# A hybrid decoder layer on one core: every tensor in SBUF at another address

## The chip, the cores and the metric

The kernel runs on one core of a Trainium2 chip. The metric is the device time of the whole program in microseconds (us), from one launch to its end; lower is better. Beside the timed runs there is one profiled execution, from which all rows come.

## The reference

One layer of a decoder trunk on a sequence of 1024 positions with 1024 channels, in float32. Cut to what matters:

```python
hn   = rms_norm(x, norm_mix)
proj = hn @ w_in + b_in            # 1024 x 9728: x_rnn, z_rnn, q/k/v of 12 heads, z_att, two gates
xc   = causal_depthwise_conv(x_rnn)                    # 4 taps, 1280 channels
y_rnn = rg_lru(xc, ...) * silu(z_rnn)                  # block-diagonal gates, a scan over time
att  = merge of dilated_window_attention, 3 groups x 4 heads, dilations 1, 4, 16
y_att = att * silu(z_att)
merged = gates[0] * (y_rnn @ w_o_rnn) + gates[1] * (y_att @ w_o_att)
x = x + merged @ w_out
x = x + sigmoid(rms_norm(x) @ w_ple_gate + b) * (p @ w_ple)
```

## The kernel before, in words

Every large product is made from three passes. Each float32 operand is cut into a high part in TensorE's float32r format and the rest of it (`..._hi`, `..._lo`), and `passes` (lines 1144, 1148 and 1149) multiplies high by high, high by low and low by high. One pass is a weight load of 128 x 128 values and a matmul with 512 moving columns.

Weights come from HBM in 221 pieces of 128 x 512. SyncE loads them into `raw` (4 buffers, line 428 and 451), GpSimd cuts them (line 469 makes the high part, line 465 the low part) into `ring`, which has 16 slots (12 in the attention stage). TensorE gives a slot back when its last pass has started.

The stages follow one another in TensorE's program: 16 matmuls on zeros in `warm` (line 1208); transposes of the normed input, whose parts go to `hn_hi` and `hn_lo`; ten recurrent blocks j (projections with `hn` moving and weights stationary, then the gate products of `xc_hi` and `xc_lo`; VectorE and ScalarE do the convolution, the gates and the scan, and ScalarE spills `y_hi` and `y_lo` to HBM); 72 slots of q, k and v, where `hn` is stationary and the weights move. There dilation group 0 takes 128 adjacent positions of `hn` as a stationary block, group 1 takes every fourth position and group 2 every eighth. The attention steps (transposes at line 1256 and 1276, scores at 1267, values at 1287) are laid between these blocks in an order written out by hand. Then come 40 slots of gates and z, whose gates go to HBM through `g_out`; the output products in three stages of 16 (stationary weights, moving `ya`, `yra`, then `yrb` and `yrc`), for which ScalarE's queue loads the gates into `g_in` and the spilled y into `yra`, `yrb`, `yrc`; `w_out`; and the last products with `m_hi`, `m_lo`, `pT_hi`, `pT_lo`, whose results leave through `fin`.

All waits are semaphores set by hand. Nothing in the program reads an address, or waits because of one.

SBUF is laid out by hand too. `at(name, shape, dt, off)` places a tensor at `base + off`, the same in all 128 partitions, and tensors of stages that are over are overlaid. The offsets hang on a few marks: `H` (hn and what follows it there), `RW` (`raw`), `R` (`ring`), `E` (the attention stage's tensors, from ring slot 12 on), `X` (all else), `C` (small constants). In this build the first free byte (`nc.sbuf_base`) is 16481, so `base` is 16896, a multiple of 512.

Of the kernel before, what the change touches and what calls it, by code (L numbers as in the profile page):

```python
# [7 lines left out]
F32 = mybir.dt.float32  # L8
F32R = mybir.dt.float32r
# [3 lines left out]
P = 128  # L13
S = 1024
D = 1024
HALF = 512
# [3 lines left out]
NJ = RNN // P  # L20
# [26 lines left out]
RAW = 4  # L47
# [131 lines left out]
def build_layer(nc, a):  # L179
    stack = ExitStack()  # L180
    with stack:
# [1 line left out]
            return stack.enter_context(nc.semaphore(name))  # L183


        base = (nc.sbuf_base + 511) // 512 * 512

        def at(name, shape, dt, off):
            return nc.alloc_sbuf_tensor_at(name, shape, dt, offset=base + off)

        H, RW = 0, 65536
        R = RW + RAW * HALF * 4
        E = R + RING_Q * 2 * HALF * 4
        X = R + RING * 2 * HALF * 4
        C = X + 71680

        ident = at("ident", [P, P], F32, C)
        bias_in = at("bias_in", [P, 76], F32, C + 512)
        chan = at("chan", [P, 8, NJ], F32, C + 832)
        gain_mix = at("gain_mix", [P, KD], F32, C + 1152)  # L200
        eps_t = at("eps_t", [P, 1], F32, C + 1184)
        ssq_x = at("ssq_x", [P, NT], F32, C + 1216)
        std_x = at("std_x", [P, NT], F32, C + 1248)
# [1 line left out]
        half_x = at("half_x", [P, NT], F32, C + 1440)  # L205
        c_pos = at("c_pos", [P, NJ], F32, C + 1312)
        c_neg = at("c_neg", [P, NJ], F32, C + 1376)
        sp_t = at("sp_t", [P, 6, NJ], F32, X + 66560)

        hn_hi = at("hn_hi", [P, KD, S], F32R, H)  # L210
        hn_lo = at("hn_lo", [P, KD, S], F32R, H + 32768)
        ring = at("ring", [P, RING, 2, HALF], F32R, R)
        raw = at("raw", [P, RAW, HALF], F32, RW)
# [11 lines left out]
        a2buf = at("a2buf", [P, S], F32, X + 28704)  # L225
        ibuf = at("ibuf", [P, 2, S], F32, X + 32800)
        sgbuf = at("sgbuf", [P, 2, S], F32, X + 40992)
        y_hi = at("y_hi", [P, S], F32R, X + 49664)
        y_lo = at("y_lo", [P, S], F32R, X + 53760)
        xc_hi = at("xc_hi", [P, S], F32R, X + 57856)  # L230
        xc_lo = at("xc_lo", [P, S], F32R, X + 61952)

        qkv = at("qkv", [P, 3, NT, CHUNK, HD], F32, E)
        qkT = at("qkT", [P, 2, S], F32, E + 49152)
# [1281 lines left out]
```

## Time and profile before

| | |
|---|---|
| median of 3 runs | 1381.62 us (1379.93 to 1383.23) |
| the profiled execution's own time | 1379.93 us |
| its span, first to last instruction | 1378.1 us |
| TensorE busy | 1357.6 us (99%) |
| VectorE busy | 846.1 us (61%) |
| GpSimd busy | 490.5 us (36%) |
| ScalarE busy | 455.5 us (33%) |
| DMA, mean over the span | 101 GB/s |
| TensorE's granted clock, mean | 0.999 |

The profile calls TensorE's matmuls PE and its weight loads PEld, VectorE DVE, ScalarE ACT, GpSimd POOL. Matmuls are pipelined, so the duration of one is longer than the distance from its start to the next one's; it is that distance that counts for the time.

### The profile page before, as it was taken

To read this page: it belongs to the slowest core of one execution; us is meant where nothing else is said; L and a number is where in the kernel's file an instruction comes from. 1 tells how busy PE (TensorE), PEld (TensorE's weight loads), DVE (VectorE), ACT (ScalarE), POOL (GpSimd) and SP (SyncE) were. 2 spreads that over 40 slices of the span, in tenths; PEclk is the share of its full clock that TensorE was granted. 3 is DMA by queue.
4 is the path that set the end of the run, shared out by engine and by line. 5 is a ranking of instruction groups with operands and counts; after the bars stand their busy time and mean duration, and the time that the engine had idled before them with its cause. 6 is when DMAs were issued, how large, how long until landed. Compare 5 with 4: busy or idle time off the path is not lost.

```text
span 1378.1 us, 17897 instructions
## 1 busy us (share of the span) xinstructions
PE 1357.6 (99%) x6254; PEld 1168.1 (85%) x6254; DVE 846.1 (61%) x1674; ACT 455.5 (33%) x1157; POOL 490.5 (36%) x448
## 2 busy tenths in 40 slices
PE   8899999999999999999999999999999999999998
PEld 6688888888788999999999888888888788888887
DVE  6999998843768677685867774048612457235323
ACT  7354646532433343333423377211100001223100
POOL 6765424504404133040413432334057326044020
PEclk9999999999999999999999999999999999999999
DMA  6322222322202021120212132365459744221111
GB/s 241 93 84 77 95 74 77 107 94 70 77 8 85 19 90 55 38 78 16 84 39 60 63 108 87 109 207 200 139 191 412 250 132 131 92 77 52 48 46 46
DMA packets 76137, 139.51 MB, mean 101 GB/s; under 512 B 9649, under 2 KB 28817, under 8 KB 76049
## 3 DMA queue, kind: packets, MB, share of 16 engines
q10 hardware_dynamic: 31840, 75.56, 15.1%
q1 hardware_dynamic: 44208, 62.82, 15.0%
q8 instruction: 50, 0.82, 0.3%
q14 instruction: 39, 0.31, 0.1%
HBM read 108.84 MB, written 29.51 MB: 100 GB/s over the span
## 4 chain that ended last, share of the span: by engine, by line
PE 89%; DVE 7%; DMA 1%; issue 1%; ACT 1%; POOL 0%; POOLq 0%; DVEq 0%; ACTq 0%
PE bank L1144 28%; PE bank L1149 27%; PE bank L1148 27%; PE bank L1287 2%; PE bank L1267 2%; PE bank L1256 1%; DVE qkr L972 1%; DMA g_in<-gate_dram 1%; DVE qkn L957 1%; DVE qks L969 1%; PE bank L1276 1%; DVE qks L970 1%; DVE xc L872 1%; PE bank L1378 1%; DVE qkr L968 0%
## 5 line engine op out<-in xcount | busy, mean ns | idle before, releaser
L465 POOL TENSOR_TENSOR ring<-raw,ring 128x512 fp32r<-128x512 f32 x221 | 315.2, 1426 | 824.4 <-PE bank L1149 766.1
L1144 PE MATMUL bank<-hn_hi,ring 128*128 128x512 f32 x640 | 251.7, 393 | 1.2 <-DVE hn_lo L816 1.2
L1149 PE MATMUL bank<-hn_hi,ring 128*128 128x512 f32 x640 | 249.4, 390 | 0.0
L1148 PE MATMUL bank<-hn_lo,ring 128*128 128x512 f32 x640 | 249.1, 389 | 0.0
L1144 PE MATMUL bank<-ring,hn_hi 128*128 128x512 f32 x576 | 244.1, 424 | 0.2 <-POOL ring L465 0.2
L1148 PE MATMUL bank<-ring,hn_hi 128*128 128x512 f32 x576 | 229.6, 399 | 0.0
L1149 PE MATMUL bank<-ring,hn_lo 128*128 128x512 f32 x576 | 229.5, 398 | 0.0
L469 POOL TENSOR_SCALAR ring<-raw 128x512 fp32r<-128x512 f32 x221 | 181.6, 822 | 7.7 <-DMA raw<-in_w_rnn_s 7.7
L1148 PEld LDWEIGHTS bank<-ring,hn_hi 128*128 128x128 f32 x576 | 160.3, 278 | 7.1
L1149 PEld LDWEIGHTS bank<-ring,hn_lo 128*128 128x128 f32 x576 | 159.1, 276 | 7.7
L1144 PEld LDWEIGHTS bank<-ring,hn_hi 128*128 128x128 f32 x576 | 158.5, 275 | 7.6 <-POOL ring L465 0.6
L1144 PEld LDWEIGHTS bank<-hn_hi,ring 128*128 128x128 f32 x640 | 120.4, 188 | 25.5 <-POOL ring L465 1.4
L1149 PEld LDWEIGHTS bank<-hn_hi,ring 128*128 128x128 f32 x640 | 120.1, 188 | 25.4
L1148 PEld LDWEIGHTS bank<-hn_lo,ring 128*128 128x128 f32 x640 | 120.3, 188 | 24.4
L849 DVE TENSOR_TENSOR qkv<-bank,bias_qkv 128x512 f32<-128x512 f32 x72 | 49.6, 690 | 138.7 <-PE bank L1149 138.6
L579 ACT ACTIVATE sq_junk<-qkv 128x128 f32<-128x128 f32 x192 | 57.5, 300 | 158.0 <-DVE qkv L849 145.3
L1144 PE MATMUL bank<-ring,m_hi 128*128 128x512 f32 x256 | 100.4, 392 | 0.0
L1149 PE MATMUL bank<-ring,m_lo 128*128 128x512 f32 x256 | 99.7, 389 | 0.0
L1148 PE MATMUL bank<-ring,m_hi 128*128 128x512 f32 x256 | 99.6, 389 | 0.0
L617 ACT ACTIVATE probs<-scores,neg_max 128x128 f32<-128x128 f32 (+1 forms) x96 | 43.4, 452 | 134.4 <-DVE neg_max L983 134.2
L957 DVE SCALAR_TENSOR_TENSOR qkn<-qkv,rstd_qk,gain_qk 128x128 f32<-128x128 f32 x192 | 83.3, 475 | 0.4
L980 DVE CUSTOM_DVE_ANT_0 scores<-bank,masks 128x128 f32<-128x128 f32 (+1 forms) x96 | 33.3, 347 | 47.8 <-PE bank L1267 47.8
(176 smaller groups left out, 2129.2 us busy)
## 6 DMA issues: line engine op xcount, KB each, us to landing
raw<-in_w_tail_s SPq DMA_DIRECT2D x104, 256.0 KB, 2.7
g_in<-gate_dram ACTq DMA_DIRECT2D x48, 256.0 KB, 3.0
raw<-in_w_rnn_s SPq DMA_DIRECT2D x45, 256.0 KB, 2.6
raw<-in_w_qkv_s SPq DMA_DIRECT2D x48, 192.0 KB, 2.4
gate_dram<-g_out ACTq DMA_DIRECT2D x32, 256.0 KB, 2.1
raw<-in_w_qkv_s SPq DMA_DIRECT2D x48, 128.0 KB, 2.2
o_dram<-o_buf ACTq DMA_DIRECT2D x24, 256.0 KB, 2.0
o_in<-o_dram ACTq DMA_DIRECT2D x12, 512.0 KB, 4.1
```

The costliest lines, as they stand in the source:

```text
L465: nc.gpsimd.tensor_tensor(ring[:, ring_slot(p), 1], raw[:, p % RAW], ring[:, ring_slot(p), 0].bitcast(F32), ALU.subtract).then_inc(w_ready, 1)
L469: nc.gpsimd.tensor_scalar(ring[:, ring_slot(p), 0], raw[:, p % RAW], 1.0, 1.0, ALU.mult, ALU.mult).then_inc(hi_cut, 1)
L579: ins = nc.scalar.activation(sq_junk[:, i], qkv[:, c % 3, s, b], ACT.Square, accum_out=ssq_qk[:, u % HEADS, s, x:x + 1])
L617: nc.scalar.activation(probs[:, g % 2, c0:], scores[:, g % 2, c0:], ACT.Exp, bias=neg_max[:, g:g + 1], accum_out=den[:, g:g + 1]).then_inc ...
L849: V.tensor_tensor(qkv[:, c % 3, s].rearrange("p b d -> p (b d)"), bank[(N_A + T) % 4][:], bias_qkv[:, c % 2], ALU.add).then_inc(qkv_done, 1)
L957: ins = V.scalar_tensor_tensor(qkn[:, w].rearrange("p a b -> p (a b)"), qkv[:, c % 3, s, b], rstd_qk[:, s, w:w + 1], gain_qk[:, grp, w], A ...
L980: link(V.tensor_tensor_reduce(out=scores[:, g % 2, c0:], in0=bank[5][:, c0:2 * P], in1=masks[:, c0:2 * P] if grp < 2 else masks[:, 2 * P:] ...
L1144: ins = T.matmul(out, lhs[0], rhs[0], start=first, stop=False)
L1148: T.matmul(out, lhs[0], rhs[1], start=False, stop=False)
L1149: return T.matmul(out, lhs[1], rhs[0], start=False, stop=last)
L1267: T.matmul(bank[5][:, 0 if prev else P:2 * P], qkT[:, 0, tile * P:(tile + 1) * P], qkT[:, 1, k0:(tile + 1) * P], start=True, stop=True).th ...
L1287: ins = T.matmul(bank[7][:, 0:P], qkv[:, c % 3, tile - 1 + b, vb], probsT[:, g % 2, b * P:(b + 1) * P], start=b == parts[0], stop=b == 1)
```

## The change

The change moves tensors in SBUF. It rounds the base to 32 bytes instead of 512, puts the small constants (1728 bytes from mark C on, with `sp_t` now among them) between `raw` and `ring` instead of behind everything, and places `y_hi`, `y_lo`, `xc_hi` and `xc_lo` 32 bytes further up within their region.

```diff
-        base = (nc.sbuf_base + 511) // 512 * 512
+        base = (nc.sbuf_base + 31) // 32 * 32
...
-        R = RW + RAW * HALF * 4
+        C = RW + RAW * HALF * 4
+        R = C + 1728
         E = R + RING_Q * 2 * HALF * 4
         X = R + RING * 2 * HALF * 4
-        C = X + 71680
...
-        sp_t = at("sp_t", [P, 6, NJ], F32, X + 66560)
+        sp_t = at("sp_t", [P, 6, NJ], F32, C + 1472)
...
-        y_hi = at("y_hi", [P, S], F32R, X + 49664)
-        y_lo = at("y_lo", [P, S], F32R, X + 53760)
-        xc_hi = at("xc_hi", [P, S], F32R, X + 57856)
-        xc_lo = at("xc_lo", [P, S], F32R, X + 61952)
+        y_hi = at("y_hi", [P, S], F32R, X + 49696)
+        y_lo = at("y_lo", [P, S], F32R, X + 53792)
+        xc_hi = at("xc_hi", [P, S], F32R, X + 57888)
+        xc_lo = at("xc_lo", [P, S], F32R, X + 61984)
```

With 16481 as the first free byte, `base` becomes 16512. What each tensor's start leaves over when it is divided by 512, worked out from these offsets:

| tensors | before | after |
|---|---|---|
| `hn_hi`, `hn_lo`, `raw`, `yra`, `yrb`, `m_hi`, `pT_hi`, `pT_lo`, `ident` | 0 | 128 |
| `ring`, `x_nat`, `qkv`, `qkT`, `qkn`, `qkr`, `o_buf`, `ya_hi`, `yrc`, `m_lo`, `msum`, `g_in`, `fin` | 0 | 320 |
| `xc_hi`, `xc_lo`, `y_hi`, `y_lo` | 0 | 352 |
| `xc`, `rbuf`, `tbuf`, `abuf`, `a2buf`, `ibuf`, `sgbuf`, `warm` | 32 | 352 |
| `g_out`, `bias_qkv` | 192 | 0 |

## Rows read from the trace of the kernel before

**Rows 1.** The page: span; busy time, share, instructions; chain that ended last, by engine.

```profile
span 1378.1 us, 17897 instructions
...
PE 1357.6 (99%) x6254; PEld 1168.1 (85%) x6254; DVE 846.1 (61%) x1674; ACT 455.5 (33%) x1157; POOL 490.5 (36%) x448
...
PE 89%; DVE 7%; DMA 1%; issue 1%; ACT 1%; POOL 0%; POOLq 0%; DVEq 0%; ACTq 0%
```

**Rows 2.** Line 1144 over the whole span: length, PE busy (count), clock, DMA share, GB/s.

```profile
0.00:1378.10 1378.10, 712.11 (x1768) 1.00 0.30 101
```

**Rows 3.** Timeline of PE in attention group 0, first and last of 29 passes: start, duration.

```profile
299.46 0.39 PE L1144 MATMUL bank<-ring,hn_hi 128*128 128x512 f32 x1
...
305.81 0.39 PE L1148 MATMUL bank<-ring,hn_hi 128*128 128x512 f32 x1
```

**Rows 4.** Timeline of PE in groups 1 (6 passes) and 2 (12 passes).

```profile
454.94 0.39 PE L1144 MATMUL bank<-ring,hn_hi 128*128 128x512 f32 x1
...
456.11 0.40 PE L1149 MATMUL bank<-ring,hn_lo 128*128 128x512 f32 x1
...
639.69 0.41 PE L1144 MATMUL bank<-ring,hn_hi 128*128 128x512 f32 x1
...
642.40 0.41 PE L1149 MATMUL bank<-ring,hn_lo 128*128 128x512 f32 x1
```

**Rows 5.** The warm-up matmuls: all 16, then single ones by start.

```profile
1.31 6.03 PE L1208 MATMUL bank<-warm 128*128 128x512 bf16 x16 [1.31 <-POOL warm L459]
...
1.71 0.63 PE L1208 MATMUL bank<-warm 128*128 128x512 bf16 x1
...
5.98 0.50 PE L1208 MATMUL bank<-warm 128*128 128x512 bf16 x1
...
6.31 0.38 PE L1208 MATMUL bank<-warm 128*128 128x512 bf16 x1
...
6.96 0.38 PE L1208 MATMUL bank<-warm 128*128 128x512 bf16 x1
```

**Rows 6.** Groups by line and shape, VectorE and ScalarE: busy us, mean ns | idle before.

```profile
L849 DVE TENSOR_TENSOR qkv<-bank,bias_qkv 128x512 f32<-128x512 f32 x72 | 49.6, 690 | 138.7 <-PE bank L1149 138.6
...
L1113 DVE TENSOR_TENSOR fin<-bank,bias_ple 128x512 f32<-128x512 f32 x16 | 11.1, 691 | 68.0 <-PE bank L1149 68.0
...
L546 ACT ACTIVATE rbuf<-bank,chan 128x512 f32<-128x512 f32 x20 | 13.8, 690 | 3.3 <-DVE ibuf L905 3.3
...
L507 ACT ACTIVATE hn_hi<-bank,gain_mix 128x512 fp32r<-128x512 f32 x16 | 9.8, 689 | 5.0 <-PE bank L1185 4.9
```

**Rows 7.** Waits: engine line <- what it waited for: us in total, times, longest.

```profile
POOL ring L465 <- PE bank L1149: 766.1, 71, 48.1
...
PE bank L1144 <- POOL ring L465: 0.2, 1, 0.2
```

**Rows 8.** 1024 to 1080 us: length, PE, PEld, DVE, ACT, POOL busy, clock, DMA share, GB/s.

```profile
1024.00:1080.00 56.00, 56.00 (x248) 46.37 (x248) 13.09 (x19) 0.00 (x0) 38.07 (x41) 1.00 1.04 408
```

**Rows 9.** Timeline where that stretch ends: a gate load in the chain, VectorE and TensorE.

```profile
1064.43 16.61 DMA g_in<-gate_dram
...
1081.06 0.69 DVE L1062 TENSOR_TENSOR g_in<-bank,g_in 128x512 f32<-128x512 f32 x1 [12.24 <-DMA g_in<-gate_dram]
...
1080.50 0.39 PE L1149 MATMUL bank<-yra,ring 128*128 128x512 f32 x1
1081.81 0.50 PE L1144 MATMUL bank<-yra,ring 128*128 128x512 f32 x1 [0.92 <-DVE g_in L1062]
```

**Rows 10.** DMA, 3.0 us around one store of `o_buf`: its queue, share of 16 engines; landing.

```profile
q10 hardware_dynamic: 144, 0.26, 22.6%
...
o_dram<-o_buf ACTq DMA_DIRECT2D x1, 256.0 KB, 2.0
```

**Rows 11.** The same around one store of `g_out`, from 881.4 us.

```profile
q10 hardware_dynamic: 144, 0.26, 23.3%
...
gate_dram<-g_out ACTq DMA_DIRECT2D x1, 256.0 KB, 2.0
```

**Rows 12.** Timeline of the end: the last two stores are issued.

```profile
1374.39 1.67 ACTq L791 DMA_DIRECT2D out<-fin  x2
1374.99 0.69 DVE L1125 TENSOR_TENSOR fin<-fin,x 128x512 f32<-128x512 f32 x1
```

## The prediction

> **What bounds the kernel now.** First the page's busy times, then the chain that ended last: TensorE is busy for 99% of the span and makes up 89% of the chain; VectorE is 7% of it [rows 1]. So the time is the number of TensorE's instructions by the distance between them, plus a few waits. Line 1144, one of the three passes, runs 1768 times [rows 2]; lines 1148 and 1149 run as often, so there are 5304 passes. Their distance is read from starts in the timeline. In attention group 0 it is (305.81 - 299.46) / 28 = 0.2268 us [rows 3]; 5304 x 0.2268 = 1203 us, 87% of the span. 512 columns at 2.4 GHz, the level that the granted clock of 1.00 [rows 2] stands for, are 0.2133 us, so 0.0135 us per pass is something else. Because every pass counts, the question for a change of addresses is whether a pass, a packet or a vector instruction depends on where its operand begins. What a third of a nanosecond per pass is worth (5304 x 0.0003 = 1.6 us) shows how sharp that question is.
>
> **The change part by part.** Instructions, semaphores, queues and DRAM addresses stay the same; only starts in SBUF move. Nothing is added to any queue, so no wait moves behind another. What can change is the length of single pieces of work. By kind:
>
> TensorE, the weight load. A block of 128 x 128 values is 512 bytes of a partition when its columns are adjacent, 2048 bytes in group 1 and 4096 in group 2. The distance of passes is (456.11 - 454.94) / 5 = 0.234 us in group 1 and (642.40 - 639.69) / 11 = 0.2464 us in group 2 [rows 4]. So how the operand lies does reach the time: 0.0072 us for three more stretches of 512 bytes, 0.0196 us for seven, 0.0024 to 0.0028 us for each. Today no float32r operand of a matmul starts inside such a stretch except by the strides; after the change all do. If what counts were the aligned stretches that a block touches, each pass would pay one more: 5304 x 0.0028 = 14.9 us. That is the upper bound. The lower is nothing, or a gain: operands that share a start modulo 512 could as well collide today.
>
> TensorE, an operand off the boundary. The nearest row is the warm-up: `warm` is both operands and starts 32 bytes past a multiple of 512, the same remainder modulo 64 that `xc_hi` gets. At the first pace its starts run from 1.71 to 5.98 in ten steps, 0.427 us each, and 512 columns at 1.2 GHz are 0.4267 us; at the second from 6.31 to 6.96 in three steps, 0.217 us each, against 0.2133 at 2.4 GHz [rows 5]. A start off the boundary costs 0.000 us at one pace and at most 0.003 us at the other, where passes on the boundary have 0.0135. It is bf16, not float32r, so it doesn't settle the matter, but it is the nearest row: I take 0.
>
> VectorE, ScalarE. The same shapes stand in the table with different starts: the copy at line 849 reads `bias_qkv` (192 past the boundary) in 690 ns, line 1113 reads `bias_ple` (on it) in 691; ScalarE writes `rbuf` (32 past) in 690 ns and `hn_hi` (on it) in 689 [rows 6]. I take 0. The bound is 1 ns in 690, 0.15%: of VectorE's 7% of the chain (96 us) that is 0.1 us either way. If VectorE were slower all the same, that share is the cover that is gone: 1% would cost 1 us.
>
> GpSimd. All its operands (`raw`, `ring`) lie on the boundary today, so no row shows it otherwise. It waited 766.1 us for TensorE to give slots back; TensorE waited for it once, for 0.2 us [rows 7]. Busy for 490.5 us, it could be 3% slower (15 us) inside that idle time. I take 0; were the cover gone, up to those 15 us would show.
>
> DMA, reading SBUF. Two stores of 256 KB, each alone on the engines: 22.6% of 3.0 us on 16 engines is 10.85 us of packet time for `o_buf` (on the boundary), 23.3% is 11.18 us for `g_out` (192 past) [rows 10, 11]. So a store from off the boundary takes 3.1% more. Here a rule of the Trainium skill can be held against the rows. Its page "DMA: Bandwidth & Descriptors", section "How a descriptor splits into AXI transactions", says that a transaction begins at a multiple of 256 bytes, and that bytes ahead of the descriptor's start are fetched and thrown away; by its count a 2048-byte row from 192 past needs 70 beats instead of 64, an estimate of 9%, where the rows show 3.1%. After the change `g_out` is on the boundary and `o_buf`, `y_hi`, `y_lo` and `fin` are off it. All these stores end long before anyone reads them, but the last: `out<-fin` issued near 1376 us [rows 12] ends the program. A store takes 2.0 us to land, of it 3.1% is +0.06 us.
>
> DMA, writing SBUF. From 1024 to 1080 us all 16 engines are busy, at 408 GB/s, with `yra`, `yrb`, `yrc`, weights, x and gates [rows 8]. This is the one place where DMA sets the end: a gate load takes 16.61 us, VectorE waits 12.24 us for it, and TensorE starts 1.31 us after the pass before instead of 0.23, so 1.08 us are lost [rows 9]. Everything that makes this stretch longer is passed on in full. The loads' sources in DRAM do not move; their targets go from 0 to 128 or 320 past the boundary. No row that I have prices a target off it. Bounds: nothing, or what a source costs: 3.1% of 56 us = +1.7 us. Below, at most the 1.08 us come back. I take 0, because the row with a price shows the reading side.
>
> Sum: 1379.93 + 0.06 = 1380.0 us for the profiled execution (1378.1 of span and 1.8 around it). The median of the runs lies 1.69 us above that execution, so 1381.7 us.
>
> **The rivals.**
>
> Slower, at the passes. Each operand off the boundary touches one more stretch of 512 bytes, at 0.0028 us: 1381.7 + 14.9 = 1396.6 us. For it: the distances in groups 1 and 2. Against: the warm-up, and that a weight load in group 1 may be slow because of its stride and not of its length. It decides from 0.0005 us per pass on, where 2.8 us (0.2%) are reached.
>
> A longer saturated stretch. +1.7 us: 1383.4 us, still within 0.2%. If the skill's count of beats held for targets too (it is given for reads of HBM or SBUF, and HBM's addresses don't move), a 2048-byte row at 128 past would take 68 beats for 64, an estimate of 6.25% by that page. As a mechanism of this kernel it is the same row: the stretch that TensorE already waits for grows, and each per cent of it is 0.56 us. It decides from 5% on (2.8 us). At the page's figure the sum would be 3.5 us more, 1385.2 us; by that rule, the trace gives less than it says where it can be held against it (3.1% for 9%).
>
> Faster. All matmul operands share their start modulo 512 today, and `hn` and `ring` would differ by 192 after the change. If that sharing made the 0.0135 us of each pass, a tenth less of it is 5304 x 0.00135 = 7.2 us: 1374.5 us. For it: the warm-up, off the boundary, has only 0.003 us there. Against: it is another type, and its two operands are the same tensor, so they share every start, and it is still the faster.
>
> That the change does nothing to the machine at all, which is my forecast, is also the case in which it "doesn't do what it says".
>
> **How the numbers follow.** No effect that can be measured: 0.78. Slower passes: 0.08. Longer saturated stretch: 0.08, half of it large enough to count. Faster: 0.06. A measurement of this kernel can tell about 0.2% (2.8 us) from no change: three runs spread over 3.3 us. So of the 0.78, I put 0.02 on each side for chance. Same: 0.74 + 0.04 + 0.01 (a gain of the 1.08 us only) = 0.79. Slower: 0.02 + 0.08 + 0.04 = 0.14. Faster: 0.02 + 0.05 = 0.07. The range: below, the lowest run less the 1.08 us that can come back, 1378.8; above, the highest run plus 1.7 for the stretch, 0.1 for VectorE and 0.06 for the last store, 1385.1. Rounded outward, 1378.5 to 1385.5. It leaves out the slower passes (0.08) and most of the faster case (0.05).
>
> **What would show it.** In the trace of the changed kernel: the distance of passes near 300 us still 0.2268 us, near 455 us 0.234 and near 640 us 0.246; the warm-up, now 352 past, at the same paces; lines 849 and 546 still at 690 ns, with the remainders exchanged; a store of `g_out` at 22.6% and one of `o_buf` at 23.3% of its 3 us, which would show that the 3.1% is the start's; the same 408 GB/s around 1050 us and TensorE's stop near 1081 us within 1 us of its length. The prediction is wrong if the distance of passes differs by more than 0.0005 us, if that stop grows by over 3 us, or if GpSimd's instructions grow so far that TensorE waits for `ring`.

## The result, and the profile after

| | before | after |
|---|---|---|
| median of the runs | 1381.68 us (1379.93 to 1383.23) | 1399.39 us (1397.88 to 1401.54), 4 runs |
| span of the profiled execution | 1378.1 us | 1398.2 us |
| granted clock, mean | 0.999 | 0.996 |

The changed kernel is slower: ratio 1.0132, 95% interval 1.0114 to 1.0148. The forecast was 1381.7 us, in a range to 1385.5; the time lies 13.9 us above that range. The medians are 17.7 us apart; the two profiled executions, whose parts are added up below, are 20.1 us apart, since the one of before (1379.93 us) is the fastest of its runs.

The page of the changed kernel, against [rows 1]: span, busy times, chain by engine.

```profile
span 1398.2 us, 17897 instructions
...
PE 1376.3 (98%) x6254; PEld 1171.5 (84%) x6254; DVE 849.2 (61%) x1674; ACT 455.4 (33%) x1157; POOL 490.5 (35%) x448
...
PE 85%; DVE 8%; DMA 5%; issue 1%; ACT 1%; ACTq 0%; DVEq 0%
```

As many instructions, 20.1 us more of span, and 18.7 of them are TensorE's busy time. VectorE is up by 3.1 us, ScalarE and GpSimd by nothing. DMA rises from 1% to 5% of the chain. So there are two questions: why TensorE is busy for longer at the same work, and what DMA does in the chain. (Most of the 5% is no time lost: the chain now runs back through seven gate loads, from 1030 us to the stop at 1093 us, while TensorE is busy beside them. What counts is the last of them.)

The timeline of the changed kernel in attention group 0, against [rows 3]; the first and the last of 16 passes:

```profile
308.66 0.39 PE L1144 MATMUL bank<-ring,hn_hi 128*128 128x512 f32 x1
...
312.15 0.40 PE L1144 MATMUL bank<-ring,hn_hi 128*128 128x512 f32 x1
```

(312.15 - 308.66) / 15 = 0.2327 us, where [rows 3] have 0.2268. The duration of one, 0.39 us, tells nothing; the distance does. But it isn't the same everywhere. The timeline of the changed kernel at four more places (gates and z; output products; `w_out`; the last products):

```profile
900.07 0.39 PE L1144 MATMUL bank<-hn_hi,ring 128*128 128x512 f32 x1
...
922.96 0.39 PE L1148 MATMUL bank<-hn_lo,ring 128*128 128x512 f32 x1
...
1027.11 0.40 PE L1144 MATMUL bank<-ya_hi,ring 128*128 128x512 f32 x1
...
1048.91 0.39 PE L1144 MATMUL bank<-ya_hi,ring 128*128 128x512 f32 x1
...
1185.14 0.39 PE L1144 MATMUL bank<-ring,m_hi 128*128 128x512 f32 x1
...
1207.54 0.39 PE L1144 MATMUL bank<-ring,m_hi 128*128 128x512 f32 x1
```

With 100, 96 and 96 steps between these pairs: `hn` moving 0.2289 us, `ya` moving 0.2271, `ring` moving 0.2333. In the kernel before all such stretches have 0.2267 (for `hn`, 900.08 to 922.74 in 100 steps; for `ring` with `m`, 1175.14 to 1196.90 in 96). `ring` starts at 320 past a multiple of 512 in all three, and `ya` does too: this kind of pass has both operands off the boundary and costs nothing. That is the first hint of the cause.

Groups 1 and 2 against [rows 4]: 0.2386 us (461.61 to 463.28, seven steps) for 0.234, and 0.2467 for 0.2464. The strided passes of group 2 have next to nothing to lose.

The second part. TensorE's stop where the saturated stretch ends, in the changed kernel, against [rows 9], and the gate load in its chain:

```profile
1091.06 0.40 PE L1149 MATMUL bank<-yra,ring 128*128 128x512 f32 x1
1093.75 0.51 PE L1144 MATMUL bank<-yra,ring 128*128 128x512 f32 x1 [2.29 <-DVE g_in L1062]
...
1093.00 0.69 DVE L1062 TENSOR_TENSOR g_in<-bank,g_in 128x512 f32<-128x512 f32 x1 [12.87 <-DMA g_in<-gate_dram]
...
1074.97 18.00 DMA g_in<-gate_dram
```

The stop is 2.69 us from start to start, 1.38 more than the 1.31 of before, and the load takes 18.00 us for 16.61. What follows the stop stands in the windows. First the kernel before, 1090 to 1100 us, and then the changed one (length, PE, PEld, DVE, ACT and POOL busy, clock, DMA share, GB/s):

```profile
1090.00:1100.00 10.00, 10.00 (x46) 8.29 (x45) 4.99 (x7) 0.00 (x0) 3.51 (x4) 1.00 0.50 147
```

```profile
50.00:60.00 10.00, 10.00 (x38) 7.99 (x37) 9.42 (x22) 0.69 (x1) 6.05 (x7) 0.83 0.31 102
...
1090.00:1100.00 10.00, 7.71 (x27) 5.87 (x26) 6.10 (x10) 0.00 (x0) 1.54 (x3) 0.83 0.62 209
```

After the longer stop the granted clock of the stretch is 0.83 in the mean, against 1.00: TensorE runs for 3.4 us of the ten at the lower of its two levels, 1.2 GHz, and loses about half of that, 1.7 us. The granted clock is lower near 55 us too (0.83, where before has 0.97). That isn't laid to the change: `raw_128` of group 3, whose passes are all as fast as before, shows the same 0.83 and the same 38 matmuls from 50 to 60 us.

Where the 20.1 us are: the distances between neighbouring starts of passes in both traces, pair by pair (5162 pairs that no wait ends), add up to 16.0 us. The stop is 1.4, the clock after it 1.7, and the stretch from 40 to 60 us, with 54 matmuls for 59, about 1.1, which can differ between executions for reasons of its own, as `raw_128` shows.

### The profile page after: what moved, and what is told of

Same layout as the page of the kernel before. It is cut to its first block, busy times and chain, and to the rows that moved or that the text cites. A ratio compares the mean times of both kernels' runs of the same rounds, so it can differ in the third digit from the quotient of the medians.

```text
span 1398.2 us, 17897 instructions
## 1 busy us (share of the span) xinstructions
PE 1376.3 (98%) x6254; PEld 1171.5 (84%) x6254; DVE 849.2 (61%) x1674; ACT 455.4 (33%) x1157; POOL 490.5 (35%) x448
## 4 chain that ended last, share of the span: by engine, by line
PE 85%; DVE 8%; DMA 5%; issue 1%; ACT 1%; ACTq 0%; DVEq 0%
PE bank L1144 26%; PE bank L1149 26%; PE bank L1148 26%; DMA g_in<-gate_dram 4%; PE bank L1287 2%; PE bank L1267 2%; DVE qkr L972 1%; DVE qkn L957 1%; PE bank L1256 1%; DVE qks L969 1%; PE bank L1276 1%; DVE qks L970 1%; DVE xc L872 1%; PE bank L1378 0%; DVE qkr L968 0%
## 5 line engine op out<-in xcount | busy, mean ns | idle before, releaser
L465 POOL TENSOR_TENSOR ring<-raw,ring 128x512 fp32r<-128x512 f32 x221 | 315.7, 1429 | 842.5 <-PE bank L1149 780.2
```

The source lines that it names most:

```text
L465: nc.gpsimd.tensor_tensor(ring[:, ring_slot(p), 1], raw[:, p % RAW], ring[:, ring_slot(p), 0].bitcast(F32), ALU.subtract).then_inc(w_ready, 1)
```

## The experiments

Two theories stood for the passes. One (A) is the rival of the prediction: what counts is where an operand itself begins. The other (R): what counts is how far the moving operand and the stationary one lie apart, modulo 256 or 512. For the rest of the time there was a third: the targets of the loads (D, from group 4 on T; its rival there is P, that the engines' own operands count). All kernels compute the whole layer. Where a ratio stands, the kernel was run 5 to 11 times; where none stands, once. The times of the kernel before beside them are 1380.80, 1381.24, 1381.06, 1382.73 and 1379.58 us in the five groups below.

### Group 1: all off the boundary, but together

`all_128`: everything moves by the same amount, to 128 past (`warm`, `xc` and the like to 160).

```diff
-        base = (nc.sbuf_base + 511) // 512 * 512
+        base = (nc.sbuf_base + 31) // 32 * 32
```

> The kernel before with only the base rounded to 32 bytes: every tensor 128 past a multiple of 512, all still equal to each other. Theory R (a pass pays when the moving operand and the weights loaded beside it start at different remainders): distance of passes 0.2267 us as before, time within 3 us of before, a longer stop near 1081 us at most. Theory A (a pass pays because its operands start off a multiple of 512): 0.230 us and more, time near the changed kernel's 1399 us. Theory D (the DMA targets off the boundary lengthen the saturated stretch by 3 to 4%): +1 to +3 us from the stop near 1081 us.

`all_32`: the same with `base` at 32 past.

```diff
-        base = (nc.sbuf_base + 511) // 512 * 512
+        base = (nc.sbuf_base + 511) // 512 * 512 + 32
```

> The kernel before with the base 32 bytes higher: every tensor 32 past a multiple of 512 (an odd multiple of 32), all still equal. Theory R: 0.2267 us per pass, time within 3 us of before. Theory A: at least as slow as the changed kernel, since 32 is the smallest multiple in use. Theory D: +1 to +3 us.

`ring_equal_128`: the changed kernel, but `ring` (and with it mark X) at 128 past, the same as `hn`. `xc`'s parts stay 32 off from it.

```diff
-        R = C + 1728
+        R = C + 1536
...
-        sp_t = at("sp_t", [P, 6, NJ], F32, C + 1472)
+        sp_t = at("sp_t", [P, 6, NJ], F32, X + 66560)
```

> The changed kernel with 1536 instead of 1728 bytes between raw and ring (sp_t back at its old offset): hn, raw, ring and all else at 128, only xc and y 32 further. Theory R: passes back at 0.2267 us but for the 120 gate passes of xc (0.233), so about 16 us of the loss are gone: 1383 to 1386 us. Theory A: no pass is nearer to the boundary, time stays at 1397 to 1400 us.

`only_xc_32`: the kernel before, and of the change only the four lines of `y` and `xc`.

> The kernel before with only y_hi, y_lo, xc_hi and xc_lo 32 bytes further up. Theory R and theory A: the 120 passes of xc at 0.233 us instead of 0.2267, all others unchanged, +0.8 us in all, which one run can't show; the distances can.

Measured: `all_128` 1384.16 us, ratio 1.0025 (1.0016 to 1.0035); `all_32` 1383.32, 1.0018 (1.0009 to 1.0028); `ring_equal_128` 1384.45, 1.0026 (1.0014 to 1.0037); `only_xc_32` 1380.76. The timeline of `all_128`, gates and z:

```profile
900.02 0.39 PE L1148 MATMUL bank<-hn_lo,ring 128*128 128x512 f32 x1
...
922.69 0.39 PE L1149 MATMUL bank<-hn_hi,ring 128*128 128x512 f32 x1
```

That is 0.2267 us in 100 steps, as before the change, with every operand 128 past the boundary. Every pass off it and none slower: theory A falls, and with it 15 of the 18 us are gone at one stroke (1399.39 - 1384.16 = 15.2). `ring_equal_128` says the same from the other side: the changed layout with one distance put right. In `only_xc_32` just the passes of `xc` differ. Its timeline:

```profile
72.01 0.40 PE L1144 MATMUL bank<-xc_hi,ring 128*128 128x512 f32 x1
...
74.58 0.40 PE L1149 MATMUL bank<-xc_hi,ring 128*128 128x512 f32 x1
```

Eleven steps, 0.2336 us each: 32 bytes apart is enough. The kernel doesn't feel it, for only 120 passes are of this kind (0.8 us).

But 3.4 us stay in `all_128` that R doesn't explain.

### Group 2: how far apart

The changed layout with `xc`, `y` and `sp_t` at their old offsets, and `ring` 64, 128 and 256 further on than `hn`; and everything together at 256 past.

```diff
         C = RW + RAW * HALF * 4
-        R = C + 1728
+        R = C + 1536 + 64       # apart_64; + 128: apart_128; + 256: apart_256
```

```diff
-        base = (nc.sbuf_base + 511) // 512 * 512
+        base = (nc.sbuf_base + 255) // 256 * 256   # all_256
```

> The changed kernel with ring and all behind it 64 bytes apart from hn in their remainder (hn and raw at 128, the rest at 192; xc and y at 192 too). Theory R: where both operands are in different regions (hn or m_hi with ring) the distance is 0.229 to 0.236 us, where both are at 192 (ya, yrc) 0.2267. Theory A: all passes alike slow, ya too.

> The same, 128 apart (hn at 128, ring at 256). Theory R with a modulus of 128 bytes: 0.2267 us everywhere, time near 1384 us. With a modulus of 256 or 512: hn with ring slow as in the changed kernel, near 1397 us.

> The same, 256 apart (hn at 128, ring at 384). Theory R with a modulus of 128 or 256: 0.2267 us everywhere, 1384 us. With a modulus of 512: slow, near 1397 us.

> The kernel before with its base at 256 past a multiple of 512, all tensors equal. Theory R: passes at 0.2267 us. Theory D with pieces of 256 bytes on the writing side: the loads' targets are on such a boundary again, 412 GB/s from 1030 to 1070 us, a stop of 0.9 to 1.3 us near 1081 us, 1380 to 1382 us. Theory D with pieces of 512 bytes: 398 GB/s, a stop of 2.8 us, 1384 us.

Measured: `apart_64` 1402.98 us, `apart_128` 1400.84, `apart_256` 1386.22, ratio 1.0040 (1.0025 to 1.0054), `all_256` 1381.88, ratio 1.0002 (0.9992 to 1.0011). The timeline of `apart_64`, once with `hn` moving and once with `ring` moving:

```profile
900.10 0.39 PE L1144 MATMUL bank<-hn_hi,ring 128*128 128x512 f32 x1
...
923.44 0.39 PE L1148 MATMUL bank<-hn_lo,ring 128*128 128x512 f32 x1
...
1191.45 0.39 PE L1144 MATMUL bank<-ring,m_hi 128*128 128x512 f32 x1
...
1213.43 0.39 PE L1144 MATMUL bank<-ring,m_hi 128*128 128x512 f32 x1
```

0.2334 us (100 steps) and 0.2290 (96 steps): the two values of the changed kernel, exchanged. There `hn` minus `ring` is 128 - 320, which is 64 modulo 256, and `ring` minus `m_hi` is 192; here they are 192 and 64. So the sign of the distance counts, and one operand, `ring`, can't be the cause by its own place. By moving minus stationary, modulo 256, from such pairs of starts:

| difference | kernels and operands | us per pass |
|---|---|---|
| 0 | before; all_128, all_32, all_256, apart_256 (256 apart); `ya` after | 0.2267 to 0.2271 |
| 32 | `xc` in only_xc_32; in ring_equal_128 and after | 0.2336; 0.2335 |
| 64 | `hn` after; `m` in apart_64 | 0.2289, 0.2290 |
| 128 | `hn` and `m` in apart_128 | 0.2323, 0.2335 |
| 192 | `m` after; `hn` in apart_64 | 0.2333, 0.2334 |

The table holds for long stretches with one difference. It doesn't hold for a few equal passes among unequal ones. In `only_xc_32` every operand but `xc` is at 0, and still the passes of `hn` right behind those of `xc` are slow:

```profile
74.81 0.40 PE L1144 MATMUL bank<-hn_hi,ring 128*128 128x512 f32 x1
...
76.66 0.39 PE L1149 MATMUL bank<-hn_hi,ring 128*128 128x512 f32 x1
...
77.34 0.39 PE L1149 MATMUL bank<-hn_hi,ring 128*128 128x512 f32 x1
```

Eight steps take 0.2313 us each, the three behind them 0.2267. In the changed kernel `yrc`, whose difference from `ring` is 0, comes in runs of six passes between nine of `yrb` (64):

```profile
1135.31 0.40 PE L1144 MATMUL bank<-yrc,ring 128*128 128x512 f32 x1
...
1136.70 0.40 PE L1144 MATMUL bank<-yrb,ring 128*128 128x512 f32 x1
```

Six steps of 0.2317 us; over all its 96 passes `yrc` has 0.2315, and 0.2307 in `y_and_raw_128` of group 3, where it is 0 from `ring` among passes 128 apart. So what passes with another difference leave behind reaches some eight passes on.

The period is 256, not 512: `apart_256` has 0.2267 us at both places. Its 5 us over the kernel before belong to the other part, as in `all_128`: its stop at 1081 us is 4.34 us long. (It was expected at 1384 us, and `apart_128` near 1397; both came out 2 to 4 us longer.)

### Group 3: whose targets

`all_256` keeps everything on a multiple of 256 and is as fast as before; `all_128` isn't. What differs is the stretch of [rows 8]. The DMA view of its full part, 1042 to 1060 us, in the kernel before, in `all_128` and in `apart_256`:

```profile
DMA packets 3079, 7.43 MB, mean 413 GB/s; under 512 B 334, under 2 KB 334, under 8 KB 3079
```

```profile
DMA packets 2939, 7.16 MB, mean 398 GB/s; under 512 B 321, under 2 KB 321, under 8 KB 2939
```

```profile
DMA packets 2904, 6.99 MB, mean 388 GB/s; under 512 B 320, under 2 KB 320, under 8 KB 2904
```

413 GB/s become 398, 3.6% less, and `apart_256` even comes to 388 (why it and not `all_128` is open). Four kernels on `base` rounded to 256: one target or two at 128 past a multiple of 256, and the changed order of the tensors with nothing off. What lies behind a moved tensor makes room by 256.

```diff
-        raw = at("raw", [P, RAW, HALF], F32, RW)
+        raw = at("raw", [P, RAW, HALF], F32, RW + 128)        # raw_128, y_and_raw_128
...
-        yra = at("yra", [P, NA, 2, S], F32R, H)
-        yrb = at("yrb", [P, 3, 2, S], F32R, H + 40960)
+        yra = at("yra", [P, NA, 2, S], F32R, H + 128)         # y_and_raw_128
+        yrb = at("yrb", [P, 3, 2, S], F32R, H + 41088)
...
-        g_in = at("g_in", [P, 3, HALF], F32, X + 65536)
+        g_in = at("g_in", [P, 3, HALF], F32, X + 65664)       # g_in_128
```

```diff
-        R = RW + RAW * HALF * 4
+        C = RW + RAW * HALF * 4                               # front_256
+        R = C + 1536
...
-        C = X + 71680
```

> The kernel all_256 with only raw, the target of the weight loads, 128 bytes further up (ring and what follows it 256). raw is no operand of a matmul. Theory R: passes 0.2267 us throughout. Theory D, by targets: the weight packets grow by about 3%, the rest not; 408 GB/s from 1035 to 1065 us and a stop of 1.3 to 2 us near 1081 us. If any load off the boundary slows its neighbours too, 398 GB/s as in all_128.

> As raw_128, and yra and yrb 128 further up too: they are targets of loads and moving operands. Theory R: only the 128 x 3 passes of yra and yrb, 128 apart from ring, at 0.229 to 0.238 us (+0.8 to +4 us), all others 0.2267. Theory D: 398 GB/s or less, since all loads but g_in and x go off the boundary.

> As all_256 with only g_in 128 further up, the target of the gate loads that VectorE waits for. Theory D: 408 GB/s, the 48 gate loads 3% longer, a stop of 1.3 to 2 us.

> The changed layout (constants between raw and ring) with the base rounded to 256, 1536 bytes between raw and ring (sp_t at its old place) and y and xc back on the boundary: every matmul operand and every target of a large load at a multiple of 256. Theories R and D: nothing left of the loss, 1380 to 1383 us, within 0.2% of before. If placing the constants in front costs anything by itself, more.

Measured: `raw_128` 1381.22 us, `g_in_128` 1381.10, `y_and_raw_128` 1382.96, `front_256` 1380.20 with ratio 0.9998 (0.9989 to 1.0007). From 1042 to 1060 us they have 413, 413, 410 and 413 GB/s. The passes of `yra` in `y_and_raw_128`, which are 128 apart from `ring`, take 0.2333 us (1082.97 to 1096.97, 60 steps). No single target brings the 398. Theory D had expected 408 for `raw_128` and `g_in_128` and 398 or less for `y_and_raw_128`; all three missed. `front_256` shows that the constants between `raw` and `ring` cost nothing by themselves: the new order of the tensors is harmless, their remainders are not.

### Group 4: targets or TensorE's operands

`all_128` moves the targets and the operands of the passes at once. `targets_128` has `base` 128 past and `ring` on a multiple of 256; `operands_128` is the same with `base` on a multiple of 256, so that all targets of the stretch are on one and `ring` is off. In both, `ring` and `hn` are 128 apart. `ya_128` moves `ya` alone. (x and `fin` move by 128 with `g_in`, and the constants make room.)

```diff
-        base = (nc.sbuf_base + 511) // 512 * 512
+        base = (nc.sbuf_base + 31) // 32 * 32      # targets_128; operands_128: 255) // 256 * 256
...
-        R = RW + RAW * HALF * 4
+        R = RW + RAW * HALF * 4 + 128
...
-        yrc = at("yrc", [P, 2, 2, S], F32R, X + 32768)
+        yrc = at("yrc", [P, 2, 2, S], F32R, X + 32896)
...
-        g_in = at("g_in", [P, 3, HALF], F32, X + 65536)
+        g_in = at("g_in", [P, 3, HALF], F32, X + 65664)
```

```diff
-        ya_hi = at("ya_hi", [P, HEADS, S], F32R, X + 32768)
-        ya_lo = at("ya_lo", [P, HEADS, S], F32R, X + 49152)
+        ya_hi = at("ya_hi", [P, HEADS, S], F32R, X + 32896)   # ya_128
+        ya_lo = at("ya_lo", [P, HEADS, S], F32R, X + 49280)
```

> All targets of the loads in the stretch (raw, yra, yrb, yrc, g_in, the first four x rows) at 128 past a multiple of 256, ring, ya and msum on it; hn and m_hi at 128 too. Theory T (targets count, in their sum): 398 GB/s from 1035 to 1065 us. Theory P (the engines' operands beside the loads count): 412 GB/s. Theory R: hn and m_hi passes at 0.233 us as in apart_128, 1397 to 1401 us.

> The reverse: all those targets on a multiple of 256, ring, ya, msum and what lies behind ring at 128 past it. Theory T: 412 GB/s. Theory P: 398 GB/s. Theory R: passes that pair hn, yra, yrb, yrc or m_hi with ring 128 apart, 0.233 us, near 1400 us; ya with ring 0.2267.

> The kernel all_256 with only ya_hi and ya_lo 128 further up: TensorE reads them during the first 40 us of the saturated stretch, no load writes them. Theory T: 412 GB/s. Theory P, if it is TensorE's moving reads: 398 GB/s and a longer stop near 1081 us. Theory R: the 192 passes of ya at 0.233 us, +1.2 us, which leaves the loads more time.

Measured: `targets_128` 1405.94 us, `operands_128` 1404.64, `ya_128` 1380.72. The slow passes are in both of the first two and take time until the stretch begins, so the window is 1056 to 1074 us. The DMA view of `targets_128`, of `operands_128`, and of the changed kernel in the same window:

```profile
DMA packets 2949, 7.17 MB, mean 398 GB/s; under 512 B 322, under 2 KB 322, under 8 KB 2949
```

```profile
DMA packets 3068, 7.43 MB, mean 413 GB/s; under 512 B 335, under 2 KB 335, under 8 KB 3068
```

```profile
DMA packets 2940, 7.16 MB, mean 398 GB/s; under 512 B 326, under 2 KB 326, under 8 KB 2939
```

The rate goes with the targets and not with the operands, though those are slower in both. Both times lie above what was expected (1397 to 1401 us and near 1400): `hn` moving against `ring` is 128 apart here and takes 0.2327 us in the mean of all its passes, where the changed kernel (64 apart) has 0.2292. The waits of TensorE for `g_in` follow, first `targets_128`, then `operands_128` (us in total, times, longest):

```profile
PE bank L1144 <- DVE g_in L1062: 2.0, 1, 2.0
```

```profile
PE bank L1144 <- DVE g_in L1062: 0.4, 1, 0.4
```

`ya_128` is a case in which slower passes cost nothing: its `ya` passes take 0.2332 us (1016.82 to 1039.21, 96 steps; 0.6 us in all), and the stop behind them is 0.4 us instead of 0.9, because TensorE arrives later at a load that lands when it did before. The cover that the prediction looked for with other engines is here.

### Group 5: how many targets

`y_raw_g_in_128` has `yra`, `yrb`, `raw` and `g_in` off a multiple of 256, and `yrc` and x on one; `y_g_in_128` puts `raw` back on one. In both, `ring` and `hn` are 128 apart.

```diff
-        base = (nc.sbuf_base + 511) // 512 * 512
+        base = (nc.sbuf_base + 31) // 32 * 32
...
-        R = RW + RAW * HALF * 4
+        R = RW + RAW * HALF * 4 + 128
...
-        raw = at("raw", [P, RAW, HALF], F32, RW)
+        raw = at("raw", [P, RAW, HALF], F32, RW + 128)        # y_g_in_128 alone
...
-        g_in = at("g_in", [P, 3, HALF], F32, X + 65536)
+        g_in = at("g_in", [P, 3, HALF], F32, X + 65664)
```

> raw, yra, yrb and g_in off a multiple of 256, yrc and the x rows on it, ring and ya on it, hn off it. Theory T by sum: as slow a stretch as targets_128 from 1040 us on, since these four carry nearly all of the bytes until 1060 us, 396 to 400 GB/s once it is full. Should only x and yrc matter: 412 GB/s. Passes as in apart_128, 1400 us or more.

> The same with raw on a multiple of 256: yra, yrb and g_in off it. Theory T by sum of bytes: in between, 400 to 405 GB/s. If every load must be off the boundary for the effect, 412 GB/s.

Measured: 1403.97 and 1402.58 us. The DMA view from 1056 to 1074 us, first with three targets off, then with two:

```profile
DMA packets 2942, 7.15 MB, mean 397 GB/s; under 512 B 318, under 2 KB 318, under 8 KB 2942
```

```profile
DMA packets 3042, 7.36 MB, mean 409 GB/s; under 512 B 335, under 2 KB 335, under 8 KB 3042
```

The effect isn't a sum, which had promised 400 to 405 GB/s for `y_g_in_128`. `raw` alone costs nothing (413), y and `raw` 3 GB/s, y and `g_in` 4, and all three together 16. `apart_128`, where `g_in` alone is on a multiple of 256, has 410 in the same window. In these runs the full loss comes only when every load that runs in the stretch has its target off a multiple of 256; y alone, and `raw` with `g_in`, weren't run. Why it is so stays open.

## Why the prediction was wrong

**What bounds the kernel.** Right: the time is the number of passes by their distance, and a third of a nanosecond per pass is 1.6 us. The mean pass became 3.1 ns longer (16.0 us / 5162).

**TensorE, an operand off the boundary: the step that failed.** "It is bf16, not float32r, so it doesn't settle the matter, but it is the nearest row: I take 0." The term measured +16.0 us, and the distance of passes near 300 us went from 0.2268 us to 0.2327, far over the 0.0005 that the prediction had named as its sign of being wrong. The doubt was about the wrong thing. The warm-up of [rows 5] is off the boundary, but its two operands are one tensor, so their difference is 0 throughout, the case that costs nothing. In the changed kernel, at 352 past, its starts go from 5.82 to 6.47 in three steps, 0.217 us again. The prediction names that fact itself, in the rival "faster", and uses it there only against a gain. The row could not show a cost of two operands that part, and the change parts them; the table of remainders in the section on the change has it plainly (128 against 320).

**The rival "slower, at the passes"** had nearly the time (1396.6 us) by another mechanism. "Each pass would pay one more" stretch of 512 bytes: `all_128` and `all_32`, in which each pass does, keep 0.2267 us. It was right for its "It decides from 0.0005 us per pass on" and for the size of one such step, 0.0028 us against the 3.1 ns measured; that the two agree is chance as far as these runs show. The "faster" rival looked at the right quantity, the starts that operands share, with the sign wrong: sharing is what makes a pass fast.

**TensorE, the weight load.** Its duration didn't change (189 ns for `ring`, 275 for `hn` in the changed kernel). The profile does show why two operands can meet at all. The timeline of the changed kernel near its end:

```profile
1392.69 0.39 PE L1149 MATMUL bank<-ring,pT_lo 128*128 128x512 f32 x1
1392.69 0.19 PEld L1144 LDWEIGHTS bank<-ring,pT_hi 128*128 128x128 f32 x1
1392.92 0.39 PE L1144 MATMUL bank<-ring,pT_hi 128*128 128x512 f32 x1
1392.92 0.19 PEld L1148 LDWEIGHTS bank<-ring,pT_hi 128*128 128x128 f32 x1
```

The weights of the next pass are loaded from the moment the matmul before it starts, so both streams read SBUF together. That they hinder each other by their relative place is a reading of the numbers, not shown: no run took the overlap away. Nor is it separated whether a pass's own weights count or the next one's: in the changed kernel the passes with `m_lo`, which differ from `ring` by 0, stand among passes that differ by 192, and the distance is 0.2333 us over all, but what earlier passes leave behind (group 2) could do that by itself.

**VectorE, ScalarE, GpSimd.** Right. In the changed kernel line 849 has 690 ns, line 1113 691, line 546 689, line 507 689, all with other remainders than in [rows 6]; GpSimd's line 465 has 1429 ns and 469 819, and it waits 780.2 us for TensorE. VectorE's 3.1 us more of busy time are not in these groups. Lines 957, 969 and 972 gain 1.4 to 2.2 us each, but their median durations are the same in both traces (346, 284 and 285 ns), so no price of an address shows there.

**DMA, reading SBUF.** `g_out`, now on the boundary, and `o_buf`, now 320 past. Two DMA views of the changed kernel, 3.0 us from 866.2 and from 540.2 us, against [rows 10, 11]:

```profile
q10 hardware_dynamic: 144, 0.26, 22.6%
...
gate_dram<-g_out ACTq DMA_DIRECT2D x1, 256.0 KB, 2.0
...
q10 hardware_dynamic: 144, 0.26, 22.7%
...
o_dram<-o_buf ACTq DMA_DIRECT2D x1, 256.0 KB, 2.0
```

`g_out` is at 22.6% as forecast, so the 3.1% were the start's. `o_buf` was expected at 23.3% and is at 22.7%: 64 past a multiple of 256 costs 0.4% (one step of the last digit shown), 192 past costs 3.1%. The price depends on how far the start lies behind the multiple, and taking one figure for all starts was too coarse; it was worth 0.06 us.

**DMA, writing SBUF: the second wrong term.** "I take 0, because the row with a price shows the reading side." Measured, 413 GB/s become 398, 3.6%, above the bound of 3.1% that the reading side gave. The forecast for such a stretch, "each per cent of it is 0.56 us", gives 2.0 us, and the stop grew by 1.38 in the changed kernel and by 1.86 in `all_128` (1081.81 to 1084.98). What the prediction lacked is what a longer stop sets off, 3.4 us at the lower clock. `all_128` shows it behind its stop of 3.17 us (mean granted clock 0.72 from 1085 to 1090 us); `all_256`, whose stop is 1.84 us, has 1.00 there. With it the whole is worth 3.4 us (`all_128` less the kernel before), so the rival "a longer saturated stretch" was there, beside the slower passes. The rule of the Trainium skill, "DMA: Bandwidth & Descriptors", section "How a descriptor splits into AXI transactions", is written of reads. If it held for targets too, a 2048-byte row at 128 past would take 6.25% more beats and a row of 4096 bytes, which carries about half of the bytes here, 3.1%: some 4.7% for the mix, an estimate by that page. The trace has 3.6%, and a single kind of target off the boundary costs nothing (413 GB/s), which the rule would not give.

**The chances.** "That the change does nothing to the machine at all" got 0.78, from one row of another type at one remainder and in one combination. No row of before has a pass of 512 columns whose two operands differ in their starts: that was the unknown. The range, by its own words, "leaves out the slower passes (0.08)"; with that bound in it, it would have gone to 1396.6 us, still 2.8 short of the measured time.

## What to carry to other kernels

In a kernel bound by back-to-back matmuls, give the moving and the stationary operand of each matmul the same start modulo 256 bytes; the common remainder itself is free. Do it for all passes that follow one another, for a few equal ones among unequal ones stay slow. Put the targets of loads that saturate DMA on a multiple of 256 bytes as well. When a nearby row is to price a change of layout, ask which differences between tensors it holds at zero, for a row in which both operands are one tensor says nothing about two that part.

## What the runs showed of the hardware

- A float32r pass of 512 columns takes 0.2267 us when its operands' starts are equal modulo 256 bytes, and 0.2289 (64), 0.2323 to 0.2335 (128), 0.2333 (192) or 0.2335 us (32) by moving minus stationary, at every pair of starts measured with that difference, in long stretches of one difference. The sign counts.
- Passes with equal starts right behind unequal ones take 0.2313 us for eight passes (`only_xc_32`), and runs of six between unequal ones never get back to 0.2267 (0.2315 for `yrc` in the changed kernel).
- Loads lose 3.6% of their rate (413 to 398 GB/s) when all that run together have targets 128 or 32 past a multiple of 256; one or two kinds of them off cost 0 to 4 GB/s. The remainder modulo 256 isn't all: `apart_256`, also with all targets at 128 past, has 388.
- After a stop of 1.31 us (the kernel before) the granted clock is 1.00, after one of 2.69 us (the changed kernel) it is at half for 3.4 us: 1.4 us more of wait cost 3.1.
- A store of 256 KB takes about 0.4% more packet time from 64 past a multiple of 256, and 3.1% from 192 past.
